# Last expert pair's down products by output halves, and the result stored from two queues

## The reference

```python
def expert_block(args):
    xblk, e = args
    hid = jax.nn.silu(xblk @ w_gate[e]) * (xblk @ w_up[e])
    return hid @ w_down[e]                       # (tokens of e, 512) @ (512, 1024)

yb = lax.map(expert_block, (xb, block_e)).reshape(n_rows, d)
y = jax.ops.segment_sum(yb * row_w[:, None], row_tok, num_segments=t + 1)[:t]
...
h = h + hierarchical_moe(...)
return rms_norm_2(h, final_g)                    # y * rsqrt(mean(y*y) + eps) * g
```

## Time and profile before

| | us |
|---|---|
| median of 3 runs | 1106.88 |
| lowest and highest | 1104.37, 1108.78 |
| the profiled execution | 1107.08 |
| its span | 1105.4 |
| TensorE busy | 1082.7 |
| VectorE busy | 617.5 |
| ScalarE busy | 402.2 |

### The profile page before, as it was taken

How to read it: one execution, slowest core, us unless ns; L and a number is a source line. 1 busy time by engine, 2 the same in 40 slices (tenths; PEclk the granted TensorE clock), 3 DMA queues, 4 the chain that set the end, 5 groups by cost and what they waited for, 6 DMA issues and landing times.

```text
span 1105.4 us, 17516 instructions
## 1 busy us (share of the span) xinstructions
PE 1082.7 (98%) x7004; PEld 801.5 (73%) x7004; DVE 617.5 (56%) x1249; ACT 402.2 (36%) x652; POOL 6.0 (1%) x21
## 2 busy tenths in 40 slices
PE   9999999999999999999999999999999999999996
PEld 6988778998899999999799994444444444444442
DVE  4999997777568888887978762221111111111112
ACT  6522336466355554546676331111111111111112
POOL 2000000000000000000000000000000000000000
PEclk9999999999999999999999989999999999999998
DMA  8544323544245767776544598999999999999994
GB/s 301 172 161 145 102 89 114 172 172 134 76 153 174 231 231 242 240 255 193 186 138 131 215 405 371 426 429 427 427 426 428 428 427 428 427 427 427 427 427 165
DMA packets 44883, 302.62 MB, mean 274 GB/s; under 512 B 5248, under 2 KB 6400, under 8 KB 30976
## 3 DMA queue, kind: packets, MB, share of 16 engines
q1 hardware_dynamic: 41616, 287.59, 67.0%
q10 hardware_dynamic: 3184, 13.87, 3.5%
HBM read 300.39 MB, written 1.05 MB: 273 GB/s over the span
## 4 chain that ended last, share of the span: by engine, by line
PE 91%; DVE 4%; ACT 2%; issue 1%; DMA 1%; SPq 0%; ACTq 0%; DVEq 0%
PE psum L1989 90%; DMA ring<-in_stream 1%; DVE w_low L1143 1%; ACT w_high L653 1%; DVE arena L1143 1%; PE psum L2773 1%; DVE rt L1146 0%; PE psum L2779 0%; DVE x L1143 0%; DVE h L1146 0%; SPq L469 0%; SPq L472 0%; DVE h_low L1143 0%; DVE h_low L1146 0%; DVE arena L1140 0%
## 5 line engine op out<-in xcount | busy, mean ns | idle before, releaser
L1989 PE MATMUL psum<-experts_held,arena 128*64 128x512 f32 x1536 | 333.6, 593 | 2.2 <-DVE scatter_turned L1139 1.0
L1989 PEld LDWEIGHTS psum<-experts_held,arena 128*64 128x64 f32 x1536 | 111.2, 137 | 212.0 <-issue 211.1
L1143 DVE TENSOR_TENSOR w_low<-ring,w_high 128x1024 fp32r<-128x1024 f32 x150 | 180.4, 1219 | 35.7 <-ACT w_high L653 35.0
L653 ACT CAST w_high<-ring 128x1024 fp32r<-128x1024 f32 x150 | 154.5, 1047 | 63.1 <-DMA ring<-in_stream 54.9
L1989 PE MATMUL psum<-h_high,w_high 128*128 128x256 f32 x528 | 133.0, 287 | 3.9 <-ACT arena L736 1.8
L1989 PE MATMUL psum<-h_low,w_high 128*128 128x256 f32 x528 | 131.0, 283 | 0.0
L1989 PE MATMUL psum<-y_high,w_high 128*128 128x256 f32 x480 | 123.1, 285 | 0.5 <-issue 0.3
L1143 DVE TENSOR_TENSOR arena<-arena,psum 128x512 f32<-128x512 f32 (+1 forms) x31 | 19.3, 631 | 182.4 <-ACT arena L1072 181.6
L1989 PE MATMUL psum<-y_low,w_high 128*128 128x256 f32 x480 | 119.6, 283 | 0.0
L1989 PEld LDWEIGHTS psum<-h_high,w_high 128*128 128x128 f32 x528 | 101.2, 192 | 6.2 <-ACT arena L736 2.0
L1989 PEld LDWEIGHTS psum<-h_low,w_high 128*128 128x128 f32 x528 | 101.2, 192 | 0.2
(11 more groups left out here) (269 smaller groups left out, 1262.4 us busy)
## 6 DMA issues: line engine op xcount, KB each, us to landing
experts_held<-in_experts SPq DMA_DIRECT2D x84, 2048.0 KB, 27.2
ring<-in_stream SPq DMA_DIRECT2D x180, 512.0 KB, 3.5
experts_held<-in_experts ACTq DMA_DIRECT2D x12, 1024.0 KB, 7.3
experts_held<-in_experts SPq DMA_DIRECT2D x12, 1024.0 KB, 12.7
x<-in_xT SPq DMA_DIRECT2D x2, 512.0 KB, 7.7
out_y<-experts_held SPq DMA_DIRECT2D x4, 256.0 KB, 3.1
arena<-in_memT SPq DMA_DIRECT2D x1, 512.0 KB, 8.8
bbd<-in_ssm_b SPq DMA_DIRECT2D x1, 512.0 KB, 11.7
```

The source lines that it names most:

```text
L653: act.copy(wh[:, high_slot(m)], ring[:, n_ % RING]).then_inc(hi_ready, 1)
L1143: return dve.tensor_tensor(o, a, b, op)
L1989: return pe.matmul(o, a, b, start=start, stop=stop, skip_group_check=True)
```

## The change

Two edits that don't depend on each other:

1. For the last pair alone, `last_downs` takes the place of `downs`. It asks for all four loads before the first matmul, then does the left half for `f` = 0 to 3, raises `down_half`, and does the right half for `f` = 0 to 3, raising `expert_used` after each `f`. The matmuls are the same 16.
2. SP stores result tiles (0,0) and (1,1) only, each after `res_vector`; ACT stores (1,0) and (0,1) from its own queue, behind both of its multiplications.

```diff
-            for tt, c in ((0, 0), (1, 0), (1, 1), (0, 1)):
-                some = slice(c * 512, c * 512 + 512)
-                sp.wait_ge(res_scalar if tt != c else res_vector, c + 1)
+            for tt in range(TT):
+                some = slice(tt * 512, tt * 512 + 512)
+                sp.wait_ge(res_vector, tt + 1)
                 sp.dma_start(out[:, tt, some], result[:, tt, some]).then_inc(s_out, 16)
             sp.wait_ge(s_out, 64)
...
+            for tt, c in ((1, 0), (0, 1)):
+                some = slice(c * 512, c * 512 + 512)
+                act.wait_ge(res_scalar, c + 1)
+                act.dma_start(out[:, tt, some], result[:, tt, some]).then_inc(s_out, 16)
...
+            def last_downs(r):
+
+                p = PAIRS - 1
+                pe.wait_ge(hT_ready, total(r, PAIRS, p + 1))
+                w = [double(r, DOWN_AT[p] + f) for f in range(FE // P)]
+                for c in range(2):
+                    for f in range(FE // P):
+                        for e in range(2):
+                            a = e * UNIT + c * 512
+                            ins = mm(dbank[c][half[e]], hT[:, f, half[e]], w[f][:, a:a + 512], f == 0, f == FE // P - 1)
+                        if c == 1:
+                            ins.then_inc(expert_used, 1)
+                    if c == 0:
+                        ins.then_inc(down_half, 1)
...
-                downs(r, PAIRS - 1)
+                last_downs(r)
```

## The result

The changed kernel took 1109.93 us (median of 12 runs, 1108.25 to 1110.91), the kernel before 1106.85 us (median of 12, 1104.37 to 1108.78). The ratio is 1.0033, with a 95% interval of 1.0024 to 1.0042: 3.7 us slower (0.0033 x 1106.85), between 2.7 and 4.6. The forecast was 1110.9 us. The result is inside the range of 1106.5 to 1113.8, and under the 0.5% that was set as "no difference", although with this many runs it is clear of zero.

What follows compares the result with a forecast made beforehand. The weights' stream holds the expert stage, TensorE just behind it. Terms 3.1 - 0.4 - 0.3 + 1.6 = +4.0 us on the profiled 1107.08 give 1111.1, forecast as 1110.9 us; 8 in 10 between 1106.5 and 1113.8.

Steps and rivals of the forecast that it cites:

- The bound and the landings: Expert stage: held by the weights' stream, TensorE just behind; load 190 lands at 1086.55, load 191 at 1089.0.
- signs of being wrong: TensorE not waiting before the last down products, load 191's landing moving, or the tail behind the products growing.
- The wait: Ahead of the last pair's first matmul: TensorE waits for load 191 until 1089.0, +3.1 us, between 2.4 and 3.1.
- The products in another order: Last pair's down products: same 16 matmuls and shapes, weights changed at every matmul either way, term 0.
- The left half early: Behind the last products: left half's scaling and low part lie beside the right half's products, -0.4 us (-0.2 to -0.5).
- The stores: Result stores at the end: two queues save only issuing time, -0.3 us, between 0 and -0.5.
- The hole: Between result stores: engines ran out of issued work; this hole of about 0.4 us can close with two queues.
- The clock: TensorE's clock likely falls to half in the new wait, slowing the down products: +1.6 us, between 0 and 3.2.
- rival 1: Last down products: same wait, but the clock holds; +2.4 us, 1109.3 us; chance 0.30.
- likeliest case: Whole kernel: the forecast with wait and clock fall, 1110.9 us, own range 1109.3 to 1112.7; chance 0.50.
- Rival 2: Last pair: load 191 lands early enough to hide the wait, only gains remain; -0.7 us, 1106.2 us; chance 0.09.
- rival 3: Last down products: clock stays low through the whole pass, 13.7 us; +9.3 us, 1116.2 us; chance 0.06.

Runs made afterwards that it cites:

- the filled one: The change plus three float32 matmuls with unused results ahead of its wait, against the kernel before: ratio 1.0023 (1.0012 to 1.0033), 2.5 us slower.
- split late: Last pair's halves split after f = 0 and 1, loads asked for at first use, against the kernel before: 1.0008 with two store queues, 0.9999 with one.
- the last pair but one: Late split in the last two pairs, against the kernel before: 0.9998 with one store queue, 0.9991 with two.
- the waits alone: Only the four load waits moved ahead, old product order and stores, against the kernel before: ratio 1.0055, then 1.0036 when run again.

## Why the prediction was right, step by step

**The bound and the landings.** Right. The stream holds the expert stage, and TensorE was released by a weight transfer in all six traces with the waits ahead. By the letter one of the prediction's own signs of being wrong did come: the landing of load 191 moved, from 1089.0 to 1086.0. But it moved by 2.3 us in the kernel before too, so the sign was ill chosen: it compared two executions and not two kernels.

**The wait, +3.1 us.** Measured 3.25 in five traces of two kernels (and 3.23 in the filled one, most of it covered). The lower bound of 2.4, taken from the moment when the last data move, was not needed: TensorE starts at the landing that the trace gives, some 0.1 us behind it (0.13 in the first trace of the change).

**The products in another order, 0.** Right: 7.09 us for the 16 matmuls in the old order, by halves (filled) and split late.

**The left half early, -0.4 us.** Measured -0.45, and by the steps named. The right half's low part still stands ahead of its scatter (0.44 us of idle time). Counted from ACT's right half, that scatter comes 0.23 us earlier (0.24 forecast) and the third square 0.35 (0.37 forecast). My own expectation for the last pair but one forgot the first of these, and was wrong by 0.6.

**The stores, -0.3 us.** Not settled: -0.3 in the mean of fourteen traces, within their scatter. Two details were wrong. The hole did not simply close: it did in the second and third traces of the change, but in the first, SP's and ACT's second issues took 1.42 and 1.51 us, as one of SP's took 1.235 before. And ACT's first store did not go later but first, at 1101.18, while ACT's second multiplication was still running. The Trainium skill, "DMA: Bandwidth & Descriptors", section "Issuing engines are not separate DMA queues", says that only issuing time is saved; the traces don't contradict it: the one with the shortest issues had one of the latest ends.

**The clock, +1.6 us.** The size came out right, 1.56 to 1.69 us in the three traces of the change, but that is luck in part: the 1.6 was the middle between nothing and the 3.2 us of one low stretch, not worked out from anything like this place. Nor did the clock fall 2.4 us after TensorE's last matmul, as it had at the end of before: it fell after about 3 us of idle time in two traces, only with the products running in the third, and in two more with the same idle time not at all. As to its chance, rival 1 (the clock holds) was seen too, in both traces of the waits alone, after the same idle time. So the rule of the Trainium skill, "TensorE: Matmul & The Clock Gate", section "HAM oscillation — how this bites in real kernels", that a wait for DMA slows what follows, held in three of five traces. Why three of three in the change and none of two in the waits alone is open. The stretch before the products is the same in both. In one of the three the fall came 0.6 us after they had begun; in the other two it was there when they began, so that there at least their order can't have set it off. It may be chance, and five traces don't tell. The two places earlier in the program, where some executions of one kernel have a fall and others none, speak for chance.

**The sum.** By the traces the change costs 3.25 + 1.62 - 0.45 = 4.4 us, before the stores; with a held clock 2.8. Timed twice it cost 3.7 (2.7 to 4.6) and 3.2 (2.1 to 4.4) us. A mixture of fallen and held clocks in the untraced runs would give that, and so would the stores' 0.3; this was not shown. The forecast was +4.0, the full price of a fall in every run. With the prediction's own chances (0.50 for a fall, 0.30 for none) a mixture would have been the better forecast, about +3.4. The likeliest case's range of 1109.3 to 1112.7 was also added up wrongly: its lower end leaves out the bounds of the wait and of the gains, and with all its own bounds (+1.4 to +6.1) it would be 1108.3 to 1113.0. Rival 2 (the wait is hidden) and rival 3 (the clock low through the whole pass) did not occur in any trace.

## What to carry to other kernels

Ask for each load where it is first used: collecting the waits ahead of a loop makes the last transfer of the list the price of the first instruction, and the landing times of a trace tell that price before anything is run (3.1 us forecast, 3.25 found). An order that gives one half early can be had without it, if the split comes late enough for the last load and early enough for the work behind it; by the traces that is worth 0.45 us here, which no timing could show. Where a stream of transfers sets the pace, measure the end from the stream's last landing, and read each run's mean clock beside its time: here runs of one kernel differ by some 4 us with it, more than such a change gives.

## What was not expected of the hardware

- The same idle time of TensorE, 3.2 us, was followed by a fall of its clock in three traces and by none in two. Where it fell, a little over 3 us of products at 1.2 GHz cost 1.6 to 1.7 us.
- ACT's queue issued a store 0.6 us before ACT's multiplication that stands ahead of it in the program was over (issue at 1101.18; the two multiplications run from 1100.43 for 1.34 us), since the semaphore it waits for had been raised by the first of them.
- One issue of a 256 KB store took from 0.35 to 1.90 us with one queue and from 0.34 to 1.71 with two, and the end of the kernel did not follow it.
- Executions of one kernel differ in whether the clock falls near 40 us and near 650 us. In 77 runs of the kernel before, those with a mean clock of 0.992 took some 3.6 us longer than those with 0.997 (1108.5 against 1104.9 in the mean).
